# The input's norm and turns by token tile, splits straight from PSUM, and first-stage weights loaded once, in a two-layer RWKV-7 and differential-attention trunk

## The reference

```
h  = rmsnorm(x, norm_g[0, 0])
dx = h_prev - h                       # h_prev: h shifted by one token
xw, xa, xg, xk = (h + dx * mix[i] for i in (1, 4, 5, 2))
w_log = -softplus(-(w0 + tanh(xw @ w1) @ w2)) - 0.5
a = sigmoid(a0 + (xa @ a1) @ a2)
g = sigmoid(xg @ g1) @ g2
k = xk @ w_rkvo[1]                    # then r, v, the recurrence, the output projection
```

## Time and profile before

| what | value |
|---|---|
| median of 3 runs | 1572.74 us (1571.31 to 1573.1) |
| span of the profiled execution | 1571.4 us; the page gives no other time of it |
| busy share | TensorE 94%, weight loads 75%, VectorE 47%, GpSimd 39%, ScalarE 37% |
| fourth tile of x in SBUF | 14.1 us from the span's start |
| ScalarE takes the first turned bank | 21.7 us |
| first mix for the gate on VectorE | 42.2 us |
| first matmul of the K projection | 79.6 us |

### The profile page before, as it was taken

How to read it: one execution, slowest core, us unless ns; L and a number is a source line. 1 busy time by engine, 2 the same in 40 slices (tenths; PEclk the granted TensorE clock), 3 DMA queues, 4 the chain that set the end, 5 groups by cost and what they waited for, 6 DMA issues and landing times.

```text
span 1571.4 us, 23524 instructions
## 1 busy us (share of the span) xinstructions
PE 1479.3 (94%) x9095; PEld 1173.8 (75%) x9095; DVE 743.0 (47%) x1133; ACT 588.2 (37%) x928; POOL 605.4 (39%) x326
## 2 busy tenths in 40 slices
PE   4899898888999999999999999988999999999998
PEld 4676577775787888888877778655778888888876
DVE  4877978856553200232148763676462200332143
ACT  5745433545232211232244434376242211232252
POOL 5343232222244443434443333334234444344432
PEclk9899899999999999999999999989999999999999
DMA  4221200031123233232332332200122333223231
GB/s 138 86 77 63 77 28 1 10 111 55 55 81 107 81 107 120 81 107 84 103 105 91 108 108 81 81 1 28 33 93 90 107 103 99 93 94 107 82 106 54
DMA packets 123503, 126.97 MB, mean 81 GB/s; under 512 B 8333, under 2 KB 120205, under 8 KB 123417
## 3 DMA queue, kind: packets, MB, share of 16 engines
q1 hardware_dynamic: 122720, 124.51, 24.5%
q0 software_dynamic: 320, 0.66, 0.2%
q10 hardware_dynamic: 376, 0.61, 0.1%
HBM read 123.64 MB, written 2.12 MB: 80 GB/s over the span
## 4 chain that ended last, share of the span: by engine, by line
PE 74%; DVE 14%; ACT 5%; issue 4%; POOL 1%; DMA 1%; ACTq 0%; SPq 0%; DVEq 0%; POOLq 0%
PE pb L561 22%; PE pb L562 21%; PE pb L563 21%; DVE xl L1872 2%; ACT whi L1346 2%; DVE tmp L2289 1%; PE pb L1245 1%; DVE inv_t L2022 1%; DVE inv_p L2020 1%; POOL wlo L466 1%; DMA xtok<-in_x_dram 1%; PE pb L1270 1%; DVE rstd L1867 1%; DVE Lg L2345 1%; PE pb L1254 1%
## 5 line engine op out<-in xcount | busy, mean ns | idle before, releaser
L463 POOL TENSOR_TENSOR wlo<-wraw,whi 128x1024 fp32r<-128x1024 f32 x108 | 262.3, 2428 | 779.5 <-ACT whi L1346 765.9
L561 PE MATMUL pb<-xh,whi 128*128 128x512 f32 x1184 | 473.5, 400 | 15.3 <-DVE xl L1872 7.9
L562 PE MATMUL pb<-xl,whi 128*128 128x512 f32 x1184 | 464.8, 393 | 0.0
L563 PE MATMUL pb<-xh,wlo 128*128 128x512 f32 x1184 | 464.8, 393 | 0.0
L1346 ACT ACTIVATE whi<-wraw 128x2048 fp32r<-128x2048 f32 (+1 forms) x111 | 209.3, 1885 | 220.4 <-PE pb L563 220.3
L561 PEld LDWEIGHTS pb<-xh,whi 128*128 128x128 f32 x1184 | 224.7, 190 | 86.7 <-issue 31.6
L466 POOL TENSOR_TENSOR wlo<-wraw,whi 128x1024 fp32r<-128x1024 f32 x111 | 275.9, 2486 | 24.3 <-ACT whi L1346 24.3
L562 PEld LDWEIGHTS pb<-xl,whi 128*128 128x128 f32 x1184 | 224.6, 190 | 47.6 <-issue 2.4
L563 PEld LDWEIGHTS pb<-xh,wlo 128*128 128x128 f32 x1184 | 224.3, 189 | 47.6
L561 PE MATMUL pb<-hid_h,whi 128*128 128x512 f32 x512 | 199.3, 389 | 0.0
L562 PE MATMUL pb<-hid_l,whi 128*128 128x512 f32 x512 | 199.2, 389 | 0.0
(11 more groups left out here) (284 smaller groups left out, 1725.9 us busy)
## 6 DMA issues: line engine op xcount, KB each, us to landing
wraw<-in_mlp_w_dram SPq DMA_DIRECT2D x128, 512.0 KB, 4.3
wraw<-in_rwkv_w_rkvo_dram SPq DMA_DIRECT2D x32, 512.0 KB, 4.3
wraw<-in_ple_w_gate_dram SPq DMA_DIRECT2D x16, 512.0 KB, 4.0
xtok<-in_x_dram SPq DMA_DIRECT2D x8, 512.0 KB, 6.4
wraw<-in_w_k_shared_dram SPq DMA_DIRECT2D x8, 512.0 KB, 4.5
wraw<-in_w_v_shared_dram SPq DMA_DIRECT2D x8, 512.0 KB, 4.4
wraw<-in_diff_w_q_dram SPq DMA_DIRECT2D x8, 512.0 KB, 4.0
wraw<-in_diff_w_o_dram SPq DMA_DIRECT2D x8, 512.0 KB, 4.4
```

What stands on the lines that cost most here:

```text
L463: pool.tensor_tensor(wlo[:, par, front], wraw[:, par, front], whi[:, par, front].bitcast(F32), ALU.subtract)
L561: mm(o, wh, ah, start=first, stop=False)
L562: mm(o, wh, al, start=False, stop=False)
L563: return mm(o, wl, ah, start=False, stop=last)
```

## The change

- **x by tile.** ScalarE takes a tile's root directly behind its squares, and an extra root of one element stands ahead of the first square. VectorE inverts and makes the diagonal by tile. TensorE turns seven feature tiles of a token tile as soon as its diagonal is there; the eighth, whose bank 7 also takes the parameters, comes at the end for all four tiles. The parameter transposes stand ahead of token tile 2's turns, the copies to `PV` ahead of tile 3's reciprocal.
- **Splits from PSUM.** ScalarE makes `xh` from the bank and `X` for the odd tiles; VectorE makes `X` for the even tiles and every `xl` from the bank, in one operation with the gain. GpSimd makes five of the eight differences, VectorE three.
- **Weights.** [w1 | a1] is loaded once; VectorE writes the mixed copy to the second half of slot 0. G1 goes to slot 1 at the start, WA2 to tiles of its own (`wa_raw`, `wa_h`, `wa_l`), also at the start. ScalarE's high parts of blocks 0 to 3 stand between the splits; `high(4)` and `high(5)` wait for fewer TensorE steps.
- **Low parts.** GpSimd keeps block 0. VectorE takes blocks 1 to 4; GpSimd goes on from block 5.
- **Moved.** GpSimd's loads of `lrow`, the second part of `cst` and `centre` wait for the fourth x tile. The lambda products on VectorE move from the start to the place before the gate's mixes.

The diff, cut to its core:

```
+DX_POOL = 5
...
             load(0, 0, [(cols(r0, P)[:, :, 0:64], w1v), (cols(r0, P)[:, :, 64:128], a1v)])
-            load(1, 1, [(cols(r1, P)[:, :, 0:64], w1v), (cols(r1, P)[:, :, 64:128], a1v)])
-            slot_free(2)
-            load(2, 0, [(cols(r0, 256)[:, :, 0:128], g1v[:, :, 0:128]),
-                        (cols(r0, 256)[:, :, 128:256], g1v[:, :, 32:160])])
-            slot_free(3)
-            load(3, 1, [(r1[0:64, 0:1024], rwkv_w2[0]), (r1[64:128, 0:1024], rwkv_a2[0])])
+            load(2, 1, [(cols(r1, 256)[:, :, 0:128], g1v[:, :, 0:128]),
+                        (cols(r1, 256)[:, :, 128:256], g1v[:, :, 32:160])])
+            sp.dma_start(wa_raw[0:64, :], rwkv_w2[0]).then_inc(s.wa_in, 16)
+            sp.dma_start(wa_raw[64:128, :], rwkv_a2[0]).then_inc(s.wa_in, 16)
...
+            pool.wait_ge(s.x_in[TT - 1], 16)
             pool.dma_start(lrow[:, :, :], bass.AP(diff_lam.tensor, diff_lam.offset, [[0, P], [HD, 4], [1, HD]]))\
...
-            for k in range(CT):
-                pool.wait_ge(s.h_ready, k + 1)
+            for k in range(DX_POOL):
+                pool.wait_ge(s.h_act if k % 2 else s.h_ready, k // 2 + 1)
...
-            low(1, 1, slice(0, 1024), True)
-            low(2, 0, slice(0, 2048), False)
-            low(3, 1, slice(0, 1024), False)
...
-            lows(N_K, N_V + 4)
+            pool.wait_ge(s.w_lo, N_K + 1)
+            pool.wait_ge(s.pe_step, 24)
+            low(N_K + 1, 1, slice(0, 2048), True)
+            lows(N_K + 2, N_V + 4)
...
+            for t in range(TT):
+                pe.wait_ge(s.x_dg, t + 1)
+                if t == 2:
                     pe.wait_ge(s.rows_in, 160)
...
+                for c in range(CT - 1):
+                    ins = input_turn(c, t)
+                    if t == TT - 1:
+                        ins.then_inc(s.x_tr, 1)
+            pe.wait_ge(s.par_ev, 2)
+            for t in range(TT):
+                ins = input_turn(CT - 1, t)
+            ins.then_inc(s.x_tr, 1)
...
+            act.wait_ge(s.small_set, 1)
+            A(small[0:1, 180:181], small[0:1, 84:85], ACT.Sqrt)
             for t in range(TT):
...
+                act.wait_ge(s.x_sq, t + 1)
+                A(x_rms[:, t:t + 1], x_ss[:, t:t + 1], ACT.Sqrt, bias=eps_n, scale=1.0 / D).then_inc(s.x_rt, 1)
             act.wait_ge(s.par_ev, 1)
+            for c in range(CT):
+                act.wait_ge(s.x_tr, c + 1)
+                A(xh[:, c, :], pb[c][:, :], ACT.Copy, scale=vec(c, V_N00)).then_inc(s.x_hi, 1)
+                if c % 2:
+                    A(X[:, c, 4:4 + S], pb[c][:, :], ACT.Copy, scale=vec(c, V_N00)).then_inc(s.h_act, 1)
+                if c == 1:
+                    act.wait_ge(s.raw0, 32)
+                    A(whi[:, 0, 0:1024], wraw[:, 0, 0:1024], ACT.Copy).then_inc(s.w_hi, 1)
+            act.wait_ge(s.w_mix, 2)
+            A(whi[:, 0, 1024:2048], wraw[:, 0, 1024:2048], ACT.Copy).then_inc(s.w_hi, 1)
             for k in range(CT):
...
                 split_high(k, St[:, V_, k, :], None, 0)
+                if k == 3:
+                    act.wait_ge(s.raw1, 32)
+                    A(whi[:, 1, :], wraw[:, 1, :], ACT.Copy).then_inc(s.w_hi, 1)
+            act.wait_ge(s.wa_in, 32)
+            A(wa_h[:, :], wa_raw[:, :], ACT.Copy).then_inc(s.w_hi, 1)
...
-            high(2, 0)
             mixes(2, 8 * 1)
...
-            high(3, 1, slice(0, 1024))
...
-            high(4, 0)
+            high(4, 0, 16)
...
             for t in range(TT):
+                if t == 3:
+                    dve.wait_ge(s.par_tr, 1)
+                    dve.tensor_copy(PV[:, :, :], pb[7][:, 0:CT * NV].rearrange("p (c v) -> p c v", v=NV)).then_inc(s.par_ev, 1)
+                    dve.tensor_copy(hv[:, 0:3], pb[7][:, CT * NV:CT * NV + 3]).then_inc(s.par_ev, 1)
+                dve.wait_ge(s.x_rt, t + 1)
+                dve.reciprocal(x_rms[:, t:t + 1], x_rms[:, t:t + 1]).then_inc(s.x_rs, 1)
...
+            def weight_low(n, dst, src, high):
+                dve.wait_ge(s.w_hi, n + 1)
+                if n == 1:
+                    dve.wait_ge(s.w_lo, 1)
+                tt(dst, src, high.bitcast(F32), ALU.subtract).then_inc(s.w_lo, 1)
...
             for k in range(CT):
-                low(k, X[:, k, 4:4 + S], k)
+                if k % 2:
+                    dve.wait_ge(s.h_act, k // 2 + 1)
+                else:
+                    dve.wait_ge(s.x_hi, k + 1)
+                    ts(X[:, k, 4:4 + S], pb[k][:, :], vec(k, V_N00), None, ALU.mult).then_inc(s.h_ready, 1)
+                stt(xl[:, k, :], pb[k][:, :], vec(k, V_N00), xh[:, k, :].bitcast(F32), ALU.mult, ALU.subtract).then_inc(s.x_ready, 1)
+                if k == 3:
+                    weight_mixes()
+            for k in range(DX_POOL, CT):
...
+                tt(St[:, V_, k, :], X[:, k, 3:3 + S], X[:, k, 4:4 + S], ALU.subtract).then_inc(s.dx_v, 1)
+            weight_low(1, wlo[:, 0, 1024:2048], wraw[:, 0, 1024:2048], whi[:, 0, 1024:2048])
             for k in range(CT):
...
                 low(k, St[:, V_, k, :], CT + k)
+                if k == 4:
+                    weight_low(2, wlo[:, 1, :], wraw[:, 1, :], whi[:, 1, :])
+            weight_low(3, wa_l[:, :], wa_raw[:, :], wa_h[:, :])
+            dve.wait_ge(s.lam_in, 16)
...
             mixes(2, MIX_G)
...
+            dve.wait_ge(s.pe_step, 16)
+            weight_low(4, wlo[:, 0, :], wraw[:, 0, :], whi[:, 0, :])
             mixes(3, MIX_K)
```

More of the change, by code:

```diff
@@ L572, in _, with input_turn @@
             pe.wait_ge(s.cst_in, 16)
-            pe.wait_ge(s.x_dg, TT)
-            for c in range(CT):
-                if c == 1:
+            def input_turn(c, t):
+                return mm(pb[c][:, t * P:(t + 1) * P], xtok[:, t, c * P:(c + 1) * P], rstd[:, t * P:(t + 1) * P],
+                          start=True, stop=True)
+            for t in range(TT):
+                pe.wait_ge(s.x_dg, t + 1)
+                if t == 2:
                     pe.wait_ge(s.rows_in, 160)
@@ L627, in _ @@
                     pe.wait_ge(s.x_ready, x_base + k + 1)
-                    three(pb[2][:, :], n, wslice(n, k * P), xs(k), n == N_W1 and k == 0, n == N_A1 and k == CT - 1)\
+                    three(pb[2][:, :], n, wslice(0, 1024 * n + k * P), xs(k), n == N_W1 and k == 0, n == N_A1 and k == CT - 1)\
                         .then_inc(s.pe_step, 1)
-            dense_block(2, 0, 0, 2, X_G)
+            pe.wait_ge(s.h_act, 1)
+            dense_block(2, 1, 0, 2, X_G)
             pe.wait_ge(s.w_lo, 4)
@@ L1340, in _, with high @@
                 act.dma_start(dst, src).then_inc(s.rows_in, 16)
[L1341 to L1346, removed]
+            def high(n, par, steps=None):
+                act.wait_ge(raw[par], 16 * (n - par))
+                act.wait_ge(s.pe_step, 8 * (n - 1) if steps is None else steps)
+                A(whi[:, par, :], wraw[:, par, :], ACT.Copy).then_inc(s.w_hi, 1)
             def split_high(k, src, gain, free):
@@ L1424, in _ @@
                 mix_high(3, g, 8 * 2)
-            high(5, 1)
+            high(5, 1, 24)
             def decay_before(c):
@@ new lines, in weight_mixes @@
+            def weight_mixes():
+                dve.wait_ge(s.raw0, 32)
+                for m, mix in ((0, MIX_W), (1, MIX_A)):
+                    w, mixed = (wraw[:, 0, 1024 * j:1024 * j + 1024].rearrange("p (k c) -> p k c", c=P)[:, :, 64 * m:64 * m + 64]
+                                for j in range(2))
+                    tt(mixed, w, PV[:, :, V_MIX + mix:V_MIX + mix + 1].to_broadcast([P, CT, 64]), ALU.mult).then_inc(s.w_mix, 1)
+            for k in range(CT):
+                if k % 2:
[6 more added lines that the diff above has]
+                    weight_mixes()
@@ L1904, in _ @@
+            for k in range(DX_POOL, CT):
+                if k % 2:
+                    dve.wait_ge(s.h_act, k // 2 + 1)
+                else:
+                    dve.wait_ge(s.h_ready, k // 2 + 1)
+                tt(St[:, V_, k, :], X[:, k, 3:3 + S], X[:, k, 4:4 + S], ALU.subtract).then_inc(s.dx_v, 1)
+            weight_low(1, wlo[:, 0, 1024:2048], wraw[:, 0, 1024:2048], whi[:, 0, 1024:2048])
             for k in range(CT):
+                if k < DX_POOL:
+                    dve.wait_ge(s.dx, k + 1)
+                else:
+                    dve.wait_ge(s.dx_v, k - DX_POOL + 1)
```

44 lines of the change are left out of this document (13 added, 31 removed).

## The result

The changed kernel takes 1564.7 us (median of 4 runs, 1563.24 to 1565.46), the kernel before on the same chip 1572.92: a ratio of 0.9947, with a 95% interval of 0.9934 to 0.9960. The forecast was 1566.2 with a range of 1563.5 to 1571.0; the median lies inside it. The profiled execution of the changed kernel has a span of 1563.5 us, 7.9 less than that of before.

What follows compares the result with a forecast made beforehand. TensorE's matmuls were taken to bound most of the span, so only the head before K's start at 79.6 could gain. Terms -6.4 + 3.8 - 5.2 + 1.3 = -6.5 took 1572.7 to 1566.2 us, range 1563.5 to 1571.0.

Steps and rivals of the forecast that it cites:

- To t0: From the start to ScalarE's first high part: 21.66 to 15.3, -6.4 (-5.0 to -7.2).
- 12.25. There the parameter transposes come first: On TensorE: tile 2's diagonal is ready at 12.25, then parameter transposes, then seven turns, ending at 15.05.
- the later of the two terms: Start of ScalarE's first high part: the later of 15.3 (TensorE's turns) and 14.5 (tile 3's landing at 12.0 + 2.5).
- t0 to M: From ScalarE's first high part to VectorE's first gate mix: 20.5 to 24.25, +3.8 (+2 to +5).
- The first rival: VectorE's PSUM readers do contend with GpSimd: 5 to 7.5 more, 1571 to 1574; chance 0.12.
- M to the end of high 4: From VectorE's first gate mix to the end of ScalarE's high part of K's weights: 25.3 before, -5.2 (-4.2 to -5.3).
- High 4 to K: From the end of ScalarE's high part of K's weights to K's start: +1.3 (0 to +1.9).
- Of that 0.7 were waits of the sigmoids for TensorE which now hide: Before K's start: of the first K split's 1.85 delay, 0.7 was sigmoid waits for TensorE that now hide.
- the second rival: TensorE at the low clock for longer, on G, WA2 or K: 1567.7 to 1569.2; chance 0.13.
- What is won there I carry to the end one to one: From K's start to the span's end: distance unchanged, so K's gain of 6.5 reaches the end in full.
- The third rival: Parameters land late, each us after 12.3 costing one; from about 19 on, 1569 to 1572.5; chance 0.06.
- the slower one: G's weights land late, at 40.1 or later for slower by over 0.2%: 1576; chance 0.05.

Runs made afterwards that it cites:

- the run with two SBUF inputs: Changed kernel, but VectorE's eight low parts of h are X minus xh, both in SBUF, instead of from the PSUM bank: 1565.42 us, ratio 0.9956.
- The kernel with x held back: Changed kernel with the loads of x held back until the parameter rows have landed: 1567.23 us, ratio 0.9973.
- its copy: Kernel before, unchanged, profiled once more: 1573.33 us (one run).
- the padded kernel: Kernel before with 46 satisfied waits (23 more VectorE instructions) added in VectorE's idle time at the start: 1570.91 us, ratio 0.9995.

## Why the prediction was right, and where it was off

**To t0, the mechanism right, the size 1.3 too large.** The x tile and the table load at tile 3 left the chain, as forecast. The step that failed is "12.25. There the parameter transposes come first": it took TensorE to be free by then. At its price of a turn ("seven turns at 2.04/8 = 0.25") the fourteen turns of the first two tiles would have ended at 12.45. But a turn is two records (64 for the 32 turns), so the eight records of the earlier trace rows are four turns of 0.51, and the fourteen took 4.89 us, from 8.95 to 13.84. The turns in two windows of the changed kernel (length, TensorE's matmuls, its weight loads, clock, DMA, GB/s):

```profile
8.95:12.20 3.25, 3.25 (x15) 3.25 (x16) 1.00 0.85 156
12.20:13.84 1.64, 1.64 (x15) 1.45 (x13) 1.00 0.83 238
```

Up to 12.2 the records start some 0.21 us apart, from there 0.11. The windows print a clock of 1.00 for both, but the trace's first clock record, at full, starts only at 12.16, and ahead of it there is none. The kernel before shows the same step, 0.21 to 0.11 at 24.9, where its first clock record starts. The 512-column matmuls of the changed kernel show the same ratio, 0.43 apart at a clock of 0.50 and 0.23 at 1.00. So, to judge by their pace, the first turns ran at the lower level. t0 follows the place of that step: in the five kernels with the deferral and the same work up to t0 it lies at 12.2, 13.1, 13.2, 13.7 and 14.4, and t0 at 16.56, 17.01, 16.97, 17.20 and 17.36. Behind the parameters the forecast's 2.0 came out by luck: the eight turns there are 16 records at the full pace.

**The deferral: its landing came true and was worth nothing that can be told.** Forecast 12.0, measured 11.57 for the landing, but the later of the two terms was TensorE's, as the working itself had it (15.3 against 14.5). Without the deferral t0 is 16.90, inside the 16.56 to 17.36 of those that have it. In the kernel before the same deferral, together with the lambda product out of the reciprocal's way, is worth 2.0 to K, and alone nothing.

**t0 to M, right (23.7 for 24.25).** The PSUM readers ran at their free 0.70 to 0.75. Here the rule from the Trainium skill ("SBUF — State Buffer", "Who interferes with whom") that a VectorE instruction with at most one SBUF input keeps clear of GpSimd (outside its 2-port modes, which the page excepts) agrees with the trace, and the run with two SBUF inputs shows the other side, 1.51 each. The first rival falls with it.

**M to the end of high 4, right (20.2 for 20.1).** The gain is where the term had it: the three mixes, with no GpSimd work beside them, took 2.07 for 6.30, and WA2's high part is gone from behind the tanh. The rest of the shift off GpSimd pays ahead of M, not in this term: giving back G's low part alone put M 3.0 later and cost 2.3 in time, and left the way from M to the end of high 4 at 20.8.

**High 4 to K, +2.0 in place of +1.3.** In this profile the step "Of that 0.7 were waits of the sigmoids for TensorE which now hide" failed: the first K split waited 1.94 for VectorE, and the sigmoids that start at 70.06 still waited 0.83 for TensorE. In that stretch the granted clock was near half. A window of the changed kernel, with the columns of the earlier trace rows:

```profile
66.60:70.00 3.40, 3.40 (x10) 2.38 (x9) 2.83 (x6) 2.63 (x5) 0.00 (x0) 0.53 0.21 72
```

The kernel with x held back does the same work in the same order, and its profile has no such stretch:

```profile
67.66 0.63 ACT L1367 ACTIVATE xh<-tmp 128x512 fp32r<-128x512 f32 x1 [1.94 <-DVE tmp L1898]
```

```profile
70.60:74.00 3.40, 3.35 (x14) 2.13 (x13) 2.81 (x5) 3.40 (x7) 0.00 (x0) 1.00 0.24 84
```

There the split waits the same 1.94, no sigmoid waits for TensorE, and the way from high 4 to K is 13.26, as it is with G's low part on GpSimd: the 13.4 of the forecast. So the term was right at full clock, and the missing 0.9 is the second rival at work, TensorE at the low clock in the WA2 groups. The profile of the kernel before has a stretch at half clock between its sigmoids too, from 69.3, but its copy, at full clock there, needs 12.0 for the way, hardly less than its 12.1.

**"What is won there I carry to the end one to one": wrong by 3 us, to the good.** Of the 7.9 us of span, 4.9 lie before K. 2.0 lie at the entry of the second MLP's loop, which in the traces of the padded kernel is a matter of VectorE's program and not of the head; in time that kernel gained 1.24, not clear of noise. The last 1.0 comes in small steps between 190 and 350 us, where only the kernel before has a stretch at half clock from 332 to 339; it is no more than one execution differs from the next (the timed spans of one kernel spread by a standard deviation of 1.1 to 2.5). The median came out at 1564.7, then, not because the terms were right to a microsecond, but because two misses, 1.6 too little in the head and 3.0 too much behind it, point opposite ways: that is luck. The third rival (late parameters) and the slower one (late G weights) did not come up: VectorE copied the parameters as soon as TensorE had turned them, and ScalarE reached G's high part at 27.86 without a wait.

## What to carry to other kernels

When a landing is brought forward, read what stands behind it on every in-order queue that it feeds: the same three deferred loads were worth nothing alone, 2.0 us with a product moved aside, and nothing that can be told once TensorE had become the later term. When an engine takes over work from a loaded one, place it where that engine waits (60.60 to 51.03 for one subtraction, 5.0 us in the end with what moved beside it), not where its operands happen to be asked for. And compare where two traces part behind the edit: a microsecond there may belong to the program's layout and the clock, and not to the edit. Before a row's time is divided by a count, find out what is counted: here a turn is two records.

## What the runs showed of the hardware

- TensorE's first turns ran at half their later pace (records 0.21 us apart, then 0.11) up to the place where the trace's first clock record starts, in all twelve traces; ahead of it the profile prints a clock of 1.00 without a record.
- Which engine loses when VectorE and GpSimd both read two SBUF operands depends on the case. In the earlier trace rows VectorE took 1.63 for 0.61; with G's low part on GpSimd, VectorE's eight back-to-back subtractions, begun 0.16 us before, ran at 0.61 and GpSimd's 2.34 became 7.00, all of the difference until VectorE's series was over. The Trainium skill ("SBUF — State Buffer", "Who interferes with whom") says that the order of issue decides who blocks, for the whole instruction; the order agrees, though here GpSimd stood still for eight instructions and not for one.
- The entry of the same loop cost VectorE 0.58 us at one length of its program and 0.23 at another, in all twelve traces (four with the long entry, eight with the short).
- TensorE's wait of 1.86 to 1.88 us near 1175 was followed by a stretch near half clock in three of the four traces that have it, one of 1.53 to 1.55 at the same place in none of eight.
- A second root between squares needed no table load: one load at 5.32 served the dummy, four squares and four roots.
